# Modulation and second gate ahead of the output projection, prompt's halves in turn, sample gathers first

## The reference

```python
def trunk_layer(x, cond, p, lam_init, pos, ctx):
    mod = (jax.nn.silu(cond) @ p['w_ada'] + p['b_ada']).reshape(-1, 1, 6 * D_MODEL)
    shift1, scale1, gate1, shift2, scale2, gate2 = jnp.split(mod, 6, axis=-1)
    h = rmsnorm(x, p['norm1']) * (1.0 + scale1) + shift1
    y, own = attention_branches(h, p, lam_init, pos, ctx)   # ends with merged @ p['w_out']
    x = x + gate1 * y
    h = rmsnorm(x, p['norm2']) * (1.0 + scale2) + shift2
    x = x + gate2 * expert_choice_ffn(h, p)
    return x, own

def expert_choice_ffn(h, p):
    aff = jax.nn.softmax((xs @ p['w_router']).astype(jnp.float32), axis=-1)
    gate, idx = lax.top_k(aff.T, cap)          # cap = 2n/16: 32 sample or 16 prompt tokens per expert
    xe = xs[idx]
    hg = jnp.einsum('ecd,edf->ecf', xe, p['w_gate'])
    hu = jnp.einsum('ecd,edf->ecf', xe, p['w_up'])
    ye = jnp.einsum('ecf,efd->ecd', jax.nn.silu(hg) * hu, p['w_down']) * gate[..., None]
    return jnp.zeros_like(xs).at[idx.reshape(-1)].add(ye.reshape(-1, d))
```

## Time and profile before

| | us |
|---|---|
| median of 3 runs | 1898.5 |
| lowest, highest | 1897.38, 1900.23 |
| span of the profiled execution (first to last instruction) | 1896.4 |
| TensorE busy | 1753.8 |
| VectorE busy | 670.7 |
| ScalarE busy | 328.3 |
| GpSimd busy | 320.0 |

### The profile page before, as it was taken

How to read it: one execution, slowest core, us unless ns; L and a number is a source line. 1 busy time by engine, 2 the same in 40 slices (tenths; PEclk the granted TensorE clock), 3 DMA queues, 4 the chain that set the end, 5 groups by cost and what they waited for, 6 DMA issues and landing times.

```text
span 1896.4 us, 21463 instructions
## 1 busy us (share of the span) xinstructions
PE 1753.8 (92%) x8548; PEld 968.6 (51%) x8548; DVE 670.7 (35%) x1375; ACT 328.3 (17%) x811; POOL 320.0 (17%) x349
## 2 busy tenths in 40 slices
PE   6999999999999988879899999999999999897886
PEld 2656877894533323233255587778844333332322
DVE  1235557742512212122132455567423121211212
ACT  2232223220201001010032322222112010100101
POOL 0225454320000000000002447533200000000000
PEclk9999999999899999999999999999999999999999
DMA  9235222149499999999962642312548999999997
GB/s 386 91 156 228 97 101 78 67 157 418 181 428 430 430 429 429 430 429 429 428 248 72 245 156 92 123 62 117 212 192 348 430 429 428 430 429 430 428 429 295
DMA packets 58289, 541.14 MB, mean 285 GB/s; under 512 B 7048, under 2 KB 7496, under 8 KB 14416
## 3 DMA queue, kind: packets, MB, share of 16 engines
q1 hardware_dynamic: 56656, 535.65, 68.2%
q0 software_dynamic: 1536, 4.13, 0.6%
HBM read 536.54 MB, written 3.21 MB: 285 GB/s over the span
## 4 chain that ended last, share of the span: by engine, by line
PE 79%; DMA 10%; DVE 4%; SPq 4%; ACT 2%; issue 1%; DVEq 0%
PE banks L2303 27%; PE banks L1867 10%; PE banks L1829 8%; PE banks L1919 7%; DMA arena<-in_w_exp 6%; PE banks L2222 4%; PE banks L1719 4%; PE banks L1891 4%; SPq L678 3%; DMA ring<-in_w_exp 3%; PE banks L2382 2%; DMA ring<-in_w_att 2%; PE banks L2092 2%; PE banks L2033 1%; PE banks L2278 1%; PE banks L2148 1%
## 5 line engine op out<-in xcount | busy, mean ns | idle before, releaser
L2303 PE MATMUL banks<-arena 128*64 128x512 f32 x1680 | 380.5, 597 | 29.2 <-DMA arena<-in_w_exp 17.3
L2303 PE MATMUL banks<-ring,arena 128*64 128x512 f32 x1392 | 314.1, 597 | 25.3 <-DMA ring<-in_w_exp 15.1
L2303 PEld LDWEIGHTS banks<-arena 128*64 128x64 f32 x1680 | 117.0, 137 | 271.0 <-issue 218.6
L2303 PEld LDWEIGHTS banks<-ring,arena 128*64 128x64 f32 x1392 | 97.3, 137 | 224.9 <-issue 178.8
L1655 DVE TENSOR_TENSOR arena<-banks,arena 32x512 f32<-32x512 f32 (+1 forms) x128 | 87.9, 687 | 266.0 <-PE banks L2303 264.7
L1829 PE MATMUL banks<-ring,arena 128*128 128x384 f32 (+1 forms) x512 | 160.0, 472 | 1.9 <-ACT arena L930 1.9
L1719 PE MATMUL banks<-arena 128*128 128x128 f32 (+3 forms) x740 | 106.6, 278 | 30.5 <-DVE arena L1640 18.6
L1719 PEld LDWEIGHTS banks<-arena 128*128 128x128 f32 (+3 forms) x740 | 82.3, 139 | 95.5 <-issue 42.1
L1829 PEld LDWEIGHTS banks<-ring,arena 128*128 128x128 f32 x512 | 96.3, 190 | 61.1 <-ACT arena L930 2.4
L1919 PE MATMUL banks<-arena,ring 128*128 128x384 f32 x384 | 126.8, 488 | 0.0
L1138 ACT ACTIVATE arena<-banks 128x512 f32<-128x512 f32 x32 | 19.1, 597 | 510.8 <-PE banks L2303 510.8
(11 more groups left out here) (251 smaller groups left out, 2045.6 us busy)
## 6 DMA issues: line engine op xcount, KB each, us to landing
arena<-in_w_exp SPq DMA_DIRECT2D x69, 2048.0 KB, 30.6
ring<-in_w_exp SPq DMA_DIRECT2D x69, 2048.0 KB, 30.0
ring<-in_w_att SPq DMA_DIRECT2D x80, 1024.0 KB, 7.0
arena<-in_w_exp SPq DMA_DIRECT2D x72, 1024.0 KB, 27.5
ring<-in_w_exp SPq DMA_DIRECT2D x36, 1024.0 KB, 13.8
ring<-in_w_att SPq DMA_DIRECT2D x26, 768.0 KB, 9.0
arena<-in_w_att SPq DMA_DIRECT2D x12, 1024.0 KB, 11.4
ring<-in_w_att SPq DMA_DIRECT2D x8, 672.0 KB, 15.1
```

What stands on the lines that cost most here:

```text
L2303: ins = pe.matmul(PS[64 * h:64 * h + 64, bank], lhs(k), slots[i][:, c0:c0 + BF], start=k == 0, stop=k == KC - 1)
```

## The change

It has four parts. In layer 0 all eight blocks of the next modulation come ahead of the output projection, and in layer 1 the second gate's product too. The prompt's projection does its first half of columns entirely, then the second, and the second sample tile's transpose comes ahead of both. All sample gathers of the first group come before the prompt's dispatch, into PSUM banks 6 and 7, and ScalarE alone evicts them; the prompt's gathers follow together. The list of slots in layer 0's passage is the same as in layer 1. VectorE clears the second output buffer (`YS[1]`) after the gathers.

```diff
-        turn = sooner + later + last_open if layer + 1 == DEPTH else sooner + last_open + later
+        turn = sooner + later + last_open
...
+        def gather_sample_bank(g, c):
+            return PS[:, 6 + c // 4, P * (c % 4):P * (c % 4) + P] if g == 0 else PS[:, 6 + c % 2, 0:P]
+        def gather_prompt_bank(g, c):
+            w = GE * CAP_P
+            return PS[:, (5, 4, 1, 3, 1, 3, 1, 3)[c], w * c:w * c + w] if g == 0 else PS[:, 6 + c % 2, P:P + w]
...
                 act.wait_ge(aa_ok.s, aa_ok.at(l, 1))
+                if l + 1 < DEPTH:
+                    act.wait_ge(gain_out.s, gain_out.at(l, 64))
+                    rows_out_first(l + 1)
...
-                if l + 1 < DEPTH:
-                    act.wait_ge(gain_out.s, gain_out.at(l, 64))
-                    rows_out_first(l + 1)
...
+                for c in range(KC):
+                    if c % 4 == 0:
+                        act.wait_ge(sample_mm.s, sample_mm.at(l, c // 4 + 1))
+                    sample_out(0, c)
                 gather_out(0)
...
                 residual(0)
                 residual(1)
-                h2_out(l, 1)
                 affinities(0)
                 positions(0)
                 residual(2)
-                if not ahead:
-                    gain_rows()
                 affinities(1)
-                nc.vector.memset(YS[1], 0.0)
...
                 gather_out(0)
+                nc.vector.memset(YS[1], 0.0)
                 gates(0)
...
-                if l + 1 < DEPTH:
-                    gain(0, KC)
-                    pe.wait_ge(shift_ok.s, shift_ok.at(l, 2))
-                    next_ada(0, 4)
+                for k in range(KC):
+                    ins = half_ada(l, "gain2", PS[:, 5], k)
+                ins.then_inc(gain_mm.s, 1)
+                if l + 1 < DEPTH:
+                    pe.wait_ge(shift_ok.s, shift_ok.at(l, 2))
+                    for k in range(KC):
+                        ins = ada_block(l + 1, 0, k, PS[:, 4])
+                    ins.then_inc(ada_mm.s, 1)
...
                 router(l, 0)
-                pair = [user_bank(l, ("out", 0, h)) for h in range(2)]
-                for k in range(KC):
-                    for h in range(2):
-                        ins = out(pair[h], 0, h, k)
+                h2_turn(l, 1)
+                for h in range(2):
+                    ps = user_bank(l, ("out", 0, h))
+                    for k in range(KC):
+                        ins = out(ps, 0, h, k)
                         if k == KC - 1:
                             ins.then_inc(user_mm.s, 1)
-                    if k % 2 and k < KC - 1:
-                        ins.then_inc(used[place[l, ("wout", k // 2)][0]].s, 1)
-                    if k == 1:
-                        h2_turn(l, 1)
-                    if k == 2:
-                        router(l, 1)
-                    if k == 3:
-                        affinity_turn(l, 0)
+                        elif h and k % 2:
+                            ins.then_inc(used[place[l, ("wout", k // 2)][0]].s, 1)
+                        if (h, k) == (0, 3):
+                            router(l, 1)
+                        if (h, k) == (1, 0):
+                            affinity_turn(l, 0)
                 owed.append(place[l, ("wout", 3)][0])
-
                 position_turn(l, 0)
-                if l + 1 == DEPTH:
-                    gain(0, 5)
                 h2_turn(l, 2)
-                if l + 1 < DEPTH:
-                    next_ada(4, 5)
-                else:
-                    gain(5, KC)
                 router(l, 2)
...
                 for c in range(2):
                     gather_sample(0, c)
                 affinity_turn(l, 1)
-                for c in range(2, 5):
+                for c in range(2, KC):
                     gather_sample(0, c)
-                next_ada(5, KC)
...
                 position_turn(l, 1)
                 pe.wait_ge(disp_ok.s, disp_ok.in_group(l, 0, 1))
                 pe.wait_ge(xn_t.s, xn_t.at(l, 3))
-                for c in range(5):
-                    gather_prompt(0, c)
...
+                for c in range(KC):
                     gather_prompt(0, c)
```

More of the change, by code:

```diff
@@ L608, in backbone @@
         gated_ok, pad_ok = sem("gated_ok", NG), sem("pad_ok", 1)
+        sample_mm = sem("sample_mm", 2)
         gather_mm, gather_act, gather_dve = sem("gather_mm", KC * NG), sem("gather_act", 4 * NG), sem("gather_dve", 4 * NG)
@@ L1503, in gain_rows @@
                     dve.wait_ge(gain_mm.s, gain_mm.at(l, 1))
-                    nc.vector.tensor_tensor(ROW0[:, 0:256], PS[:, 5 if ahead else 4, 0:256], BR[:, BF:BF + 256], ALU.add)\
+                    nc.vector.tensor_tensor(ROW0[:, 0:256], PS[:, 5, 0:256], BR[:, BF:BF + 256], ALU.add)\
                         .then_inc(gain_row.s, 1)
-                ahead = l + 1 < DEPTH
                 dve.wait_ge(g1_in.s, g1_in.at(l, 16))
                 nc.vector.memset(AFT, 1.0)
-                if ahead:
-                    gain_rows()
+                gain_rows()
                 def residual(i):
@@ L1535, in residual @@
                         .then_inc(ms_t.s, 1)
+                    if i == 1:
+                        h2_out(l, 1)
                     dve.wait_ge(root_t.s, root_t.at(l, i + 1))
@@ L2196, in _ @@
                     branch(l, 2, c)
-                def next_ada(first, last):
-                    if l + 1 < DEPTH:
-                        for k in range(first, last):
-                            ins = ada_block(l + 1, 0, k, PS[:, 4])
-                        if last == KC:
-                            ins.then_inc(ada_mm.s, 1)
-                def gain(first, last):
-                    for k in range(first, last):
-                        ins = half_ada(l, "gain2", PS[:, 5 if l + 1 < DEPTH else 4], k)
-                    if last == KC:
-                        ins.then_inc(gain_mm.s, 1)
+                for k in range(KC):
+                    ins = half_ada(l, "gain2", PS[:, 5], k)
+                ins.then_inc(gain_mm.s, 1)
                 if l + 1 < DEPTH:
-                    gain(0, KC)
                     pe.wait_ge(shift_ok.s, shift_ok.at(l, 2))
-                    next_ada(0, 4)
+                    for k in range(KC):
+                        ins = ada_block(l + 1, 0, k, PS[:, 4])
+                    ins.then_inc(ada_mm.s, 1)
                 pe.wait_ge(user_dve.s, user_dve.at(l, evacuated(USER_AT["br2", KC - 1])))
@@ L2270, in gather_sample @@
                             pe.wait_ge(xn_t.s, xn_t.at(l, 2))
-                    else:
+                    elif g:
                         freed = gather_dve if c % 2 else gather_act
-                        if g:
-                            pe.wait_ge(freed.s, freed.in_group(l, g, c // 2))
-                        elif c >= 6:
-                            pe.wait_ge(freed.s, freed.in_group(l, 0, 1))
+                        pe.wait_ge(freed.s, freed.in_group(l, g, c // 2))
                     for t in range(1, 3):
-                        settle(pe.matmul(gather_bank(g, c)[:, 0:P], XN2[:, t, P * c:P * c + P],
-                                         DD[:, t].rearrange("p e s -> p (e s)"), start=t == 1, stop=t == 2))
+                        ins = settle(pe.matmul(gather_sample_bank(g, c), XN2[:, t, P * c:P * c + P],
+                                               DD[:, t].rearrange("p e s -> p (e s)"), start=t == 1, stop=t == 2))
+                    if g == 0 and c % 4 == 3:
+                        ins.then_inc(sample_mm.s, 1)
                 def gather_prompt(g, c):
-                    pe.matmul(gather_bank(g, c)[:, P:P + GE * CAP_P], XN2[:, 0, P * c:P * c + P], DD[:, 0, :, 0:CAP_P],
+                    pe.matmul(gather_prompt_bank(g, c), XN2[:, 0, P * c:P * c + P], DD[:, 0, :, 0:CAP_P],
                               start=True, stop=True).then_inc(gather_mm.s, 1)
@@ L2324, in _ @@
                 pe.wait_ge(xn_t.s, xn_t.at(l, 3))
-                for c in range(5):
-                    gather_prompt(0, c)
-                if l + 1 < DEPTH:
-                    pe.wait_ge(mod_row.s, mod_row.at(l + 1, 1))
-                    gather_sample(0, 5)
-                gather_prompt(0, 5)
-                for c in range(6, KC):
-                    gather_sample(0, c)
+                for c in range(KC):
                     gather_prompt(0, c)
```

34 lines of the change are left out of this document (17 added, 17 removed).

## The result

| | us |
|---|---|
| kernel before, median (4 runs) | 1897.99 (1897.38 to 1900.23) |
| changed kernel, median (4 runs) | 1910.05 (1909.61 to 1913.01) |
| ratio, 95% interval | 1.0069 (1.0057 to 1.0081) |
| changed kernel, profiled run: total, span | 1910.03, 1908.2 |

The change costs 12 us; 1907.5 with a range of 1902 to 1914 was predicted. In the timelines, PE is TensorE and SPq the sync engine's queue; L1790 is line 1790 of the kernel. The stage table of the changed kernel answers to the earlier trace rows; its columns are the same.

The account below looks back on a forecast made before the run. The prediction took the expert weights' DMA stream as the bound. Layer 0 +10 and layer 1 -1 made +9 on a span of 1896.4, so 1905.4, plus 2.1 to the median: 1907.5 us, range 1902 to 1914.

Parts of the forecast that it names:

- The bound: Expert stages: the weight stream ends last; a layer's end moves by its dry spells, less 2.45 us per load already done.
- a sign of being wrong: Layer 0: the prediction is wrong if the stage's end moves with TensorE's first expert and not with the stream.
- Part 1: Layer 0, modulation blocks 4 to 7 ahead of the output projection: projection starts 8.7 us later, at 459.0.
- the middle case: Before layer 0's projection: 8.7 us later, 3.6 of work and 5.1 of waiting, without the half-clock spell's 3.4.
- Part 2: Layer 0, projection to first expert: halves in turn save 1.8 us, router to expert takes 12.5; first expert at 523.5.
- Part 3: Layer 0's slot order: slot 13 holds five loads; dry spell ends 20.1 us later, less 9.8 for four loads: +10.
- The signs: Layer 0: some 23 us of DMA waits, one long wait for the experts' line, stream full until 490, empty until 526.
- Part 4: Layer 1: gate product starts projection 2.4 us later, first expert at 1446.2, slot 6 free at 1448.0: -1 us.
- The clock: Rival, chance 0.15: half-clock spells before the projection and in the chain; layer 0 +15.5, layer 1 +1.5: 1915.5 us.
- The weights are there: Rival, chance 0.13: blocks 5 to 7 land in time, projection moves by 3.6 only; layer 0 +5: 1902.5 us.
- The stage follows TensorE: Rival, chance 0.08: the first expert's start sets each stage's end; layer 0 -4.4, layer 1 -2.2: 1891.9 us.
- If slot 13 did not hold the queue the change would gain: Rival, no chance of its own: in layer 0 ten loads would go out in the dry spell.

Follow-up runs that it names:

- e1: Changed kernel with layer 0's old list of slots (5, 4, 1, 0, 14 ahead of 2, 3, 12, 13): 1901.05 us, ratio 1.0021 to the kernel before.
- e4: Kernel before with the output weights' slots 5, 4, 1, 0 and 14 ahead of slot 11 in layer 0's list: 1897.78 us, ratio 0.9999.
- e6: Changed kernel with slot 13 last in layer 0's list and its second round of weights loaded slot by slot instead of in pairs: 1897.11 us, ratio 0.9999.
- e9: Changed kernel with only layer 0's second round of weights as single loads instead of pairs, list of slots kept: 1910.61 us, ratio 1.0068.
- e10: Changed kernel with only slot 13 put last in layer 0's list, second round still loaded in pairs: 1903.23 us, ratio 1.0028.
- e2: Kernel before with only the changed list of slots in layer 0, no engine's instructions moved: 1903.43 us, ratio 1.0031.
- e5: e4 with layer 0's second round of weights as single loads instead of pairs: 1893.32 us, ratio 0.9978 to the kernel before.
- e8: Kernel before with only layer 0's second round of weights as single loads instead of pairs: 1897.58 us, ratio 1.0001.
- e12: e7 with both halves of the prompt's projection together again, as in the kernel before: 1889.75 us, ratio 0.9956 to the kernel before.
- e7: e6 with the next modulation's blocks 5 to 7 behind the output projection's first tile, as in e3: 1892.25 us, ratio 0.9973 to the kernel before.
- e11: e7 with the second gate's product in layer 1 as filler again, behind the position turn: 1890.17 us, ratio 0.9955 to the kernel before.
- e3: Changed kernel with the next modulation's blocks 5 to 7 behind the output projection's first tile: 1903.49 us, ratio 1.0036 to the kernel before.

## Why the prediction was right, point by point

**The bound.** Right for this change: the loads hang on slot 13, and the end of layer 0's stage moves with them. But the prediction had only half of it. That a layer's end moves by what the dry spells gain or lose holds for losses; gains were given back behind the first expert (e1, e4). In those two the stage's end moved with TensorE's first expert and not with the stream, which the prediction had named as a sign of being wrong. In the changed kernel itself the two can't be told apart, since its stream restarts with the first expert.

**Part 1, projection at 459.0.** Measured 460.29. TensorE waited 3.7 us for the weights instead of 5.1, and the last two blocks were at half clock, which the middle case had left out. The bounds were 3.6 to 12.1 us later than 450.3, the measured delay is 10.0. The other kernels with all blocks ahead had it at 458.29 (e1), 458.53 (e6), 459.55 (e9) and 461.05 (e10): the half-clock spell comes and goes (e1 has none there), and that 459 lies so near the one profile of the change is partly luck. ScalarE's copy cost nothing, as said: it ran at 460.51, and its next work came at 476.96.

**Part 2, first expert at 523.5.** Measured 525.49. Of the 2.0 us, 1.3 are the projection's start, and 0.7 the way from there: 65.2 us instead of 64.5. Inside that way two errors cancel in part. The prompt's router starts 53.5 us behind the projection instead of 52.0, mostly for the half-clock piece of the projection (1.2 us), and from there to the first expert it is 11.7 us instead of 12.5. In e1, without the spell, the router starts 52.0 us behind the projection, as forecast. The size of this part's gain was read from too little. The prediction measured it against a way of 69.7 us in the one trace of before; four kernels with the same order of this passage (e2, e4, e5, e8) took 66.8. So 2.9 us of the 5.2 that were called the chain's gain were half clock in that one trace (its router took 3.60 us, in the four 1.96). And the 1.8 us given to the halves in turn weren't theirs, but the earlier copy's, as far as they were a gain at all (e12).

**Part 3, the list: stage end +10.** Measured +12.0. By the prediction's own count, the stream restarts at 527.47 instead of 505.21, 22.3 us later, less 9.8 for the four loads: 12.5. Of the predicted 10, 3.5 were the first expert's, which leaves 6.5; the stage behind the first expert grew by 455.1 - 448.6 = 6.5. The same step measures 6.7 from e1 or e10 to the changed kernel and 8.6 in e2, so the exact hit is luck in its last digit. The miss is the first expert's 5.4 for 3.5. The signs are those named: 22.2 us of waits for DMA where 23 were expected, a 60-us wait for the experts' line, the stream full for 10 of the 25 us at 480:505 and empty from there to 527.

**Part 4, layer 1: -1.** Measured -0.1. Projection +2.4 (right), output weights' first load at 1435.61 (1423.5 predicted, and 12.0 for the later layer, makes 1435.5), slot 6 free 1.6 us earlier in the layer's frame (1.0 predicted), and next to nothing came of it against the one trace of before. Why is left open.

In the five kernels with the old order here (before, e2, e4, e5, e8) the last unit starts 430.3 to 430.7 us behind slot 6's release, which is steadier than its distance from the first expert (432.7 to 433.6); that speaks for the prediction. In the nine others slot 6 comes free 2.0 us behind the first expert each time, so the two can't be told apart, and the last unit starts 431.1 to 432.6 us behind the release, later by 0.4 to 2.3.

The one trace of before is among the best of its order, too: from layer 1's first attention row to the last unit the five take 911.9 on average (910.7 to 913.5), and the seven with the gate ahead and the halves in turn 911.0 (910.2 to 911.8). By that the part gives 0.9 us, close to the forecast. What it gives away shows from e7 to e11, 3.3 us in the profiles: the projection's late start is 2.2 of it, and e7's way from projection to first expert was no shorter for the missing filler (64.65 us, in e11 63.37; other kernels of e7's order have 63.7 to 64.7).

**The sum.** Predicted +10 - 1 = +9 on the span, measured +11.8 (1908.2 - 1896.4). Some 2 us of the difference are the first expert of layer 0, the rest is layer 1.

**The rivals.** *The clock* was right in kind: the spells came, and layer 0 ended 2.0 us above the forecast, where this rival had 5.5. *The weights are there*: no, 3.7 us of waits. *The stage follows TensorE*: as a rival for this change wrong, since e2 and e3 keep a loss of 5.8 us against the kernel before with a first expert 0.1 us later than there (e3) or 4.2 earlier (e2); but with the list mended and the pairs gone (e6, e7) it is nearly what happens, and there an earlier first expert is worth what it says: e6 to e7, Tf -6.1, time -4.9. The rule cited beside it (the Trainium skill, "Perfetto Trace Analysis", Optimization Strategies: optimize the engines that block the matmul engine) agrees with e6 to e7, and with the changed kernel to e3, where the earlier first expert also frees slot 13 earlier (Tf -5.3, time -6.6). It doesn't name the order of the loads, which is what e2 pays for. *If slot 13 did not hold the queue the change would gain*: with pairs it doesn't (e10, 1903.23), and with singles it only draws level (e6); e7, with e3's edit as well, is the first to gain. That edit with the pairs kept wasn't run.

## What to carry to other kernels

In a queue that issues in order, place a load by when its buffer comes free, not by when its data is needed: here five free buffers behind one that waits for the consumer cost as much as five loads (12.3 us) where nothing else capped the stream, and 6.7 us where the pairs did. Before counting on a stream that starts earlier, look for what caps its lead (the number of buffers, and loads that need two of them at once); e4 gained nothing from 19 us of earlier start, and 4.5 us once the pairs went. And read the length of a chain from more than one execution or kernel, since a half-clock spell of 2 to 3 us can sit in the only one that you have.

## What the runs showed of the hardware

The granted clock falls to 1.2 GHz at places that differ from kernel to kernel in the same code. The same passage took 69.7 us from projection to first expert in the one trace and 66.8 in four others (e2, e4, e5, e8). The prompt's router is one of the places: 16 passes of 128x16 in 3.60 us in the one, at half clock (granted clock 0.50 at 505:509), and in 1.96 us in e2 and in e5, at full clock. The runs of one kernel spread by 3 to 7 us (e10: 1899.2 to 1906.5). In each of the twelve experiments the longer runs tend to have the lower mean granted clock, in most only weakly, so how much of the spread the spells make isn't shown. A difference of 2 us between a median of four runs and one of ten (e11 and e7) can't be told from nothing here by the medians alone.
